# Five normed blocks handed to the FFN by 32x32 turns and transfers, on a one-core two-layer trunk

## The chip, the core and the metric

The kernel runs on one core of a Trainium2 chip. It has a matrix engine (TensorE, PE in the rows; PEld is its weight load), VectorE (DVE), ScalarE (ACT), GpSimd (POOL) and SyncE (SP), which here issues most transfers. Each engine runs its own instructions in order and waits on semaphores. The metric is the device time of one execution in microseconds (us), lower is better.

## The reference

Two layers over 512 tokens of width 1024, float32. Layer 0 mixes tokens by an mLSTM, layer 1 by sliding-window attention; each is followed by a gated FFN with a short causal convolution. Norms stand before and behind every sub-layer:

```
for i in range(2):
    z = rmsnorm(h, norm_mix_pre[i])
    z = mlstm_mixer(z, ...) if i == 0 else swa_sink_mixer(z, ...)   # ends in "@ w_out"
    h = h + rmsnorm(z, norm_mix_post[i])
    z = conv_ffn(rmsnorm(h, norm_ffn_pre[i]), w_up, conv_w, conv_b, w_down)   # u = z @ w_up, then conv, silu, "@ w_down"
    h = h + rmsnorm(z, norm_ffn_post[i])
```

What matters here is the step from a mixer's output product to `rmsnorm(h, norm_ffn_pre[i])` and to the first columns of `@ w_up`.

## The kernel before

The 512 tokens are four blocks of 128 (`NB = 4`), the width is eight tiles of 128 (`KT = 8`). Each float32 product is made of three rounded ones: an operand is kept as a rounded part (`act_hi`, `w_hi`) and the rest (`act_lo`, `w_lo`); ScalarE makes the rounded part and VectorE subtracts it from the source. TensorE contracts over partitions, so an input of a projection must have its features on the partitions. A norm leaves tokens on the partitions. Each normed block `zn[:, b % 2]` (128 tokens by 1024 features) is therefore turned on TensorE: eight 128x128 matmuls against the identity, into two PSUM banks, from where `act_hi[:, :, block]` is rounded and `act_lo[:, :, block]` split.

Behind the mLSTM, `out_block(c, ...)` (matmuls at L1690 to L1692) makes the output products of block c; `turn_norm` (L1507) turns block c-1 between its parts, `norm_post`, `norm_pre` and `norm_hi` on ScalarE and `norm_post`, `norm_pre` (L958) and `norm_lo` (L964) on VectorE make the norms of block c-1. Block c+2's products wait until block c is split, since they use its banks. The FFN then starts with four units of 128 columns over the first 256 tokens (L1498 to L1500), which need blocks 0 and 1; block 3 is turned behind the third of them (`turn_last`), and the second 256 tokens follow when all four blocks are there.

Behind the attention the same is done in half turns of four matmuls (`turn`, L1884; `turn_hi` L863, `turn_lo` L1419). The order is a list of steps, `block_work(s)`, for 16 steps of four heads, two steps a pair `m`, and a last list behind them. "out" is a quarter of a block's output product, "y" the bias (`add_bias`, L952, on VectorE) and the square for the norm, "post" and "pre" the two norms, "turn" a half turn. Every engine goes through the same list and does its own part of each entry, so the order in the list is the order in each engine's queue. In a pair TensorE makes scores, mixes values for the pair before (`mix`), turns probabilities (`turn_probs`, L1851) and puts output parts between them (`filling`). Probabilities are scaled on GpSimd (L545) once VectorE has the reciprocal of their sum (`inverse`).

SP loads the FFN's weights by `ffn_loads(l)`: four units ahead, then a loop whose loads each wait until a unit's buffer is free (L427).

Of the kernel before, what the change touches and what calls it, by code (L numbers as in the profile page):

```python
# [39 lines left out]
def trunk(nc, x, x_turned, columns, m_w_in, m_gate_bias, m_w_out, a_w_in, a_sinks, a_w_out,  # L40
# [68 lines left out]
    with ExitStack() as ctx:  # L109
# [117 lines left out]
        out_done = sem("out_done")  # L227
        warm_in = sem("warm_in")
# [46 lines left out]

        def products(n):


            last = [G_MOUT + KT, G_DOWN[0] + FT, G_AOUT + KT, G_DOWN[1] + FT][n // NB] - 1
            return (w_used, counted(last)) if n % NB == NB - 1 else (y_done, n - n // NB + 1)  # L280
# [5 lines left out]
        def block_work(s):  # L286
            c, i = s // ASTEPS, s % ASTEPS
            if c < NB:
                return {0: [("y", c - 2), ("out", c - 1, 0), ("turn", c - 3, 1)],
                        1: [("out", c - 1, 1), ("post", c - 2)],  # L290
                        2: [("out", c - 1, 2), ("pre", c - 2)],
                        3: [("turn", c - 2, 0), ("out", c - 1, 3)]}[i]
            return [("y", NB - 2), ("out", NB - 1, 0), ("post", NB - 2), ("out", NB - 1, 1),
                    ("pre", NB - 2), ("turn", NB - 3, 1), ("out", NB - 1, 2), ("turn", NB - 2, 0),
                    ("turn", NB - 2, 1), ("out", NB - 1, 3), ("y", NB - 1), ("post", NB - 1),
                    ("pre", NB - 1), ("turn", NB - 1, 0), ("turn", NB - 1, 1)]

        AT_STEPS = NB * ASTEPS
        WORK = [[w for w in block_work(s) if w[1] >= 0] for s in range(AT_STEPS + 1)]
# [46 lines left out]
        def _(sp):  # L346
# [67 lines left out]

            def ffn_loads(l):
                up, down = G_UP[l], G_DOWN[l]
                w_up = f_w_up[l].rearrange("(k p) n -> p k n", p=P)
                for j in range(4):
                    load_free(up + j)
                    tile = FT * (j % 2) + j // 2  # L420
                    load(up + j, w_up[:, :, tile * P:(tile + 1) * P],
                         raw[:, j].rearrange("p (k c) -> p k c", k=KT))
                with sp.Fori(1, FT // 2) as i:
                    for j in range(4):
                        sp.wait_ge(w_lo_done, i * 4 + counted(up + j - 4))
                        tile = i * 2 + (FT * (j % 2) + j // 2)
                        nc.sync.dma_start(raw[:, j].rearrange("p (k c) -> p k c", k=KT),  # L427
                                          w_up[:, :, bass.ds(tile * P, P)]).then_inc(raw_in[j], 16)
# [122 lines left out]
        def _(act):  # L551
# [41 lines left out]

            def norm_hi(n, b, bank):

                act.wait_ge(zt_done, n - NB + 1)
                nc.scalar.copy(act_hi[:, :, b * P:(b + 1) * P],
                               ps[:, bank:bank + 2].rearrange("p a (k t) -> p (a k) t", t=P))\
                    .then_inc(z_hi, 1)
# [119 lines left out]
            for c in range(NB):  # L719
                if c >= 2:  # L720
                    norm_hi(NB + c - 2, c - 2, 4 + 2 * (c % 2))
                if c >= 1:
                    norm_post(c - 1, c - 1, 4 + 2 * ((c - 1) % 2))
                    if c == NB - 1:
                        split_hi(G_UP[0])
                if c >= 1:
                    norm_pre(NB + c - 1, c - 1)
                    if c + 1 < NB:
                        gated_hi(c + 1, 0)
                        gated_hi(c + 1, 1)  # L730
            for n in range(1, 4):
                split_hi(G_UP[0] + n)
            norm_hi(2 * NB - 2, NB - 2, 4)
            norm_post(NB - 1, NB - 1, 6)
            norm_pre(2 * NB - 1, NB - 1)
            norm_hi(2 * NB - 1, NB - 1, 6)
# [141 lines left out]
            for m in range(A_PAIRS):  # L878
# [13 lines left out]
                for s in (2 * m, 2 * m + 1):  # L892
# [3 lines left out]
                    if s + 2 < AT_STEPS:  # L896
                        probs(s + 2)
            for w in pair_work(A_PAIRS - 1, "turn"):
                work(w)
            work(("y", NB - 2))  # L900
            mixed_hi(AT_STEPS // 2 - 1)
            for w in WORK[AT_STEPS][1:]:
                work(w)
                if w == ("turn", NB - 3, 1):
                    split_hi(G_UP[1])
# [11 lines left out]
        def _(dve):  # L917
# [43 lines left out]
            def norm_lo(n, b, bank):  # L961

                dve.wait_ge(z_hi, n - NB + 1)
# [3 lines left out]
                                        ALU.subtract).then_inc(z_lo, 1)  # L967

# [254 lines left out]
            for c in range(NB):  # L1223
                if c >= 2:
                    norm_lo(NB + c - 2, c - 2, 4 + 2 * (c % 2))
# [16 lines left out]
            for n in range(1, 4):  # L1242
                split_lo(G_UP[0] + n)
            norm_lo(2 * NB - 2, NB - 2, 4)
            norm_post(NB - 1, NB - 1, 6)
            norm_pre(2 * NB - 1, NB - 1)
            norm_lo(2 * NB - 1, NB - 1, 6)
# [186 lines left out]
            def work(w):  # L1434
# [6 lines left out]
                elif w[0] == "pre":  # L1441
                    norm_pre(3 * NB + w[1], w[1])

            inverse(0)
            for m in range(A_PAIRS):
# [25 lines left out]
                if m + 1 < A_PAIRS:  # L1471
                    inverse(2 * m + 2)
            for w in pair_work(A_PAIRS - 1, "turn"):
                work(w)
            for w in WORK[AT_STEPS]:
# [3 lines left out]
                if w == ("turn", NB - 3, 1):  # L1479
                    split_lo(G_UP[1])  # L1480
                    split_lo(G_UP[1] + 1)
# [10 lines left out]
        def _(pe):  # L1492
# [212 lines left out]
            for c in range(NB):  # L1705
                if c == 0:
                    turn_heads(1)
                if c >= 2:
                    pe.wait_ge(z_lo, c - 1)
# [5 lines left out]
                if c >= 1:  # L1715
# [75 lines left out]
            def norm_blocks(n):  # L1791
                pe.wait_ge(z_lo, n)
# [4 lines left out]
            for n, lo, hi in [(n, 0, S // 2) for n in range(4)] + [(n, S // 2, S) for n in range(4)] \  # L1797
                    + [(n, 0, S) for n in range(4, 6)]:
                g = G_AIN + n
                pe.wait_ge(z_lo, NB + hi // P)  # L1800
# [131 lines left out]
            for m in range(A_PAIRS):  # L1932
                if m + 1 < A_PAIRS:
                    scores(2 * m + 3)
                    scores(2 * m + 2)
                if m >= 1:
                    mix(m - 1)
                filling(m, 0)
# [12 lines left out]
            def turned_blocks(n):  # L1951
                pe.wait_ge(t_lo, len(TURNS) - 2 * (NB - n))
# [42 lines left out]
```

## Time and profile before

| | |
|---|---|
| median of 3 runs | 1093.57 us (1093.29 to 1093.6) |
| the profiled execution | 1094.01 us |
| its span, first to last instruction | 1091.9 us |
| TensorE busy | 1085.2 us (99%) |
| VectorE, ScalarE, GpSimd busy | 535.5, 428.7, 50.3 us |
| granted TensorE clock, mean | 0.999 of full |
| transfers | 109.51 MB, 32.7% of 16 engines on SP's queue |

The busy times overlap. Matmuls are pipelined, so the durations of neighbours overlap too, and what one costs is read from the distance between starts. Times in the timelines are from the start of the span.

### The profile page before, as it was taken

To read this page: it belongs to the slowest core of one execution; us is meant where nothing else is said; L and a number is where in the kernel's file an instruction comes from. 1 tells how busy PE (TensorE), PEld (TensorE's weight loads), DVE (VectorE), ACT (ScalarE), POOL (GpSimd) and SP (SyncE) were. 2 spreads that over 40 slices of the span, in tenths; PEclk is the share of its full clock that TensorE was granted. 3 is DMA by queue.
4 is the path that set the end of the run, shared out by engine and by line. 5 is a ranking of instruction groups with operands and counts; after the bars stand their busy time and mean duration, and the time that the engine had idled before them with its cause. 6 is when DMAs were issued, how large, how long until landed. Compare 5 with 4: busy or idle time off the path is not lost.

```text
span 1091.9 us, 14755 instructions
## 1 busy us (share of the span) xinstructions
PE 1085.2 (99%) x5550; PEld 910.3 (83%) x5550; DVE 535.5 (49%) x807; ACT 428.7 (39%) x748; POOL 50.3 (5%) x51
## 2 busy tenths in 40 slices
PE   9999999999999999999999999999999999999998
PEld 8888888898888888888889987789888888888886
DVE  7544578644343434333366587564343434523344
ACT  6511456543232323222355376653323232422242
POOL 1100211000000000000000024200000000000000
PEclk9999999999999999999999999999999999999999
DMA  9332326222324232122272542022333333312231
GB/s 287 106 106 79 114 86 224 77 74 82 115 77 115 77 115 77 39 96 96 96 193 59 154 97 78 2 78 84 108 87 105 88 105 91 101 36 99 95 136 77
DMA packets 141764, 109.51 MB, mean 100 GB/s; under 512 B 22480, under 2 KB 127088, under 8 KB 141728
## 3 DMA queue, kind: packets, MB, share of 16 engines
q1 hardware_dynamic: 140720, 105.84, 32.7%
q0 software_dynamic: 864, 2.92, 0.9%
q8 instruction: 25, 0.41, 0.2%
q10 hardware_dynamic: 144, 0.26, 0.1%
q14 instruction: 11, 0.09, 0.0%
HBM read 106.87 MB, written 2.13 MB: 100 GB/s over the span
## 4 chain that ended last, share of the span: by engine, by line
PE 98%; DVE 1%; ACT 0%; issue 0%; DVEq 0%
PE ps L1498 18%; PE ps L1499 18%; PE ps L1500 18%; PE ps L1747 7%; PE ps L1745 7%; PE ps L1746 7%; PE ps L1690 3%; PE ps L1692 3%; PE ps L1691 3%; PE ps L1579 1%; PE ps L1580 1%; PE ps L1581 1%; PE ps L1838 1%; PE ps L1869 1%; PE ps L1851 1%; PE ps L1526 1%
## 5 line engine op out<-in xcount | busy, mean ns | idle before, releaser
L1498 PE MATMUL ps<-act_hi,w_hi 128*128 128x512 f32 (+1 forms) x1016 | 368.7, 363 | 0.1
L1500 PE MATMUL ps<-act_hi,w_lo 128*128 128x512 f32 (+1 forms) x1016 | 366.4, 361 | 0.0
L1499 PE MATMUL ps<-act_lo,w_hi 128*128 128x512 f32 (+1 forms) x1016 | 366.4, 361 | 0.0
L1498 PEld LDWEIGHTS ps<-act_hi,w_hi 128*128 128x128 f32 x1016 | 191.7, 189 | 31.3 <-DVE w_lo L929 0.9
L1500 PEld LDWEIGHTS ps<-act_hi,w_lo 128*128 128x128 f32 x1016 | 191.7, 189 | 29.1
L1499 PEld LDWEIGHTS ps<-act_lo,w_hi 128*128 128x128 f32 x1016 | 191.8, 189 | 29.0 <-issue 0.2
L1747 PE MATMUL ps<-w_hi,w_lo 128*128 128x512 f32 x288 | 112.0, 389 | 0.0
L1745 PE MATMUL ps<-w_hi 128*128 128x512 f32 x288 | 112.0, 389 | 0.0
L1746 PE MATMUL ps<-w_lo,w_hi 128*128 128x512 f32 x288 | 112.0, 389 | 0.0
L755 ACT ACTIVATE arena<-ps,vecs 128x512 f32<-128x512 f32 x44 | 34.3, 779 | 188.6 <-PE ps L1500 188.6
L1264 DVE SCALAR_TENSOR_TENSOR arena<-ps,vecs,arena 128x511 f32<-128x511 f32 x44 | 33.0, 750 | 144.4 <-ACT arena L755 144.4
L749 ACT CAST w_hi<-raw 128x1024 fp32r<-128x1024 f32 x80 | 83.1, 1043 | 39.4 <-PE ps L1500 39.4
L1298 DVE TENSOR_TENSOR w_lo<-raw,w_hi 128x1024 fp32r<-128x1024 f32 x32 | 39.2, 1225 | 119.9 <-ACT w_hi L780 119.9
L1256 DVE TENSOR_TENSOR w_lo<-raw,w_hi 128x1024 fp32r<-128x1024 f32 x80 | 94.1, 1218 | 0.2
L564 ACT CAST w_hi<-raw 128x1024 fp32r<-128x1024 f32 x66 | 67.9, 1045 | 64.5 <-PE ps L1581 24.7
L1273 DVE TENSOR_TENSOR arena<-ps,arena 128x512 f32 (+1 forms) x44 | 30.5, 692 | 117.1 <-PE ps L1500 113.5
L929 DVE TENSOR_TENSOR w_lo<-raw,w_hi 128x1024 fp32r<-128x1024 f32 x65 | 78.2, 1219 | 18.7 <-ACT w_hi L564 18.6
L780 ACT CAST w_hi<-raw 128x1024 fp32r<-128x1024 f32 x32 | 33.6, 1050 | 129.3 <-PE ps L1747 129.3
L1746 PEld LDWEIGHTS ps<-w_lo,w_hi 128*128 128x128 f32 x288 | 54.1, 188 | 11.3
L1747 PEld LDWEIGHTS ps<-w_hi,w_lo 128*128 128x128 f32 x288 | 54.1, 188 | 11.2
L1745 PEld LDWEIGHTS ps<-w_hi 128*128 128x128 f32 x288 | 54.1, 188 | 11.2
L759 ACT ACTIVATE arena<-arena 128x512 f32<-128x512 f32 x44 | 27.8, 632 | 79.6 <-DVE arena L1268 79.6
(209 smaller groups left out, 1219.6 us busy)
## 6 DMA issues: line engine op xcount, KB each, us to landing
raw<-in_f_w_up SPq DMA_DIRECT2D x88, 512.0 KB, 4.7
raw<-in_f_w_down SPq DMA_DIRECT2D x44, 512.0 KB, 3.3
raw<-in_m_w_in SPq DMA_DIRECT2D x23, 512.0 KB, 4.1
raw<-in_m_w_out SPq DMA_DIRECT2D x8, 512.0 KB, 3.2
raw<-in_a_w_in SPq DMA_DIRECT2D x16, 256.0 KB, 4.3
raw<-in_a_w_out SPq DMA_DIRECT2D x16, 256.0 KB, 5.1
h<-in_x SPq DMA_DIRECT2D x4, 512.0 KB, 7.4
h<-in_x_turned SPq DMA_DIRECT2D x3, 512.0 KB, 6.7
```

The lines of the kernel that those rows point to most:

```text
L564: nc.scalar.copy(w_hi[:, s], raw[:, s % 4]).then_inc(w_hi_done, 1)
L749: nc.scalar.copy(w_hi[:, 4 + s], raw[:, s]).then_inc(w_hi_done, 1)
L755: nc.scalar.activation(cv[:, t], ps[:, 2 * t], ACT.Identity, scale=taps[l][:, 2, bass.ds(f, 1)], bias=taps[l][:, 3, bass.ds(f, 1)]).then_i ...
L929: nc.vector.tensor_tensor(w_lo[:, s], raw[:, s % 4], w_hi[:, s].bitcast(F32), ALU.subtract).then_inc(w_lo_done, 1)
L1256: nc.vector.tensor_tensor(w_lo[:, 4 + s], raw[:, s], w_hi[:, 4 + s].bitcast(F32), ALU.subtract).then_inc(w_lo_done, 1)
L1298: nc.vector.tensor_tensor(w_lo[:, j], raw[:, j], w_hi[:, j].bitcast(F32), ALU.subtract).then_inc(w_lo_done, 1)
L1498: nc.tensor.matmul(dst, uh[:, k], zh, start=(k == 0), stop=False)
L1499: nc.tensor.matmul(dst, uh[:, k], zl, start=False, stop=False)
L1500: ins = nc.tensor.matmul(dst, ul[:, k], zh, start=False, stop=(k == KT - 1))
L1745: nc.tensor.matmul(dst, hi[:, bs], w_hi[:, s, hs], start=start, stop=False)
L1746: nc.tensor.matmul(dst, hi[:, bs], w_lo[:, s, hs], start=False, stop=False)
L1747: return nc.tensor.matmul(dst, lo[:, bs], w_hi[:, s, hs], start=False, stop=stop)
```

## The change

Blocks 0 to 2 behind the mLSTM and blocks 0 and 1 behind the attention (`MOVED`) are no longer turned on TensorE. VectorE turns each 32x32 piece of the block in place (`turn_squares`); SP then moves the 32-row bands to their places with 16 transfers from SBUF to SBUF of 32 partitions by 8 by 32 floats each (`move`), straight into the block's columns of `act_lo`; ScalarE rounds them into `act_hi` (`moved_round`) and VectorE subtracts (`moved_rest`). The transfers stand in SP's queue behind the first four FFN loads and ahead of the loop. Block 3 of the mLSTM side and blocks 2 and 3 of the attention side go as before.

In the attention's last list the last output part comes ahead of block 2's two turns, and in the last pair the first filling part comes ahead of `mix`. ScalarE and VectorE take the first FFN unit's weights (`split_hi`, `split_lo`) earlier in the list, and the second's behind `moved_round` and `moved_rest`. The FFN's first half waits for `moved_lo`.

```diff
+        MOVED = [(0, 0), (0, 1), (0, 2)][:3] + [(2, 0), (2, 1)][:2]
+        FIRST_MOVED = 3
@@ block_work, the last list
             return [("y", NB - 2), ("out", NB - 1, 0), ("post", NB - 2), ("out", NB - 1, 1),
-                    ("pre", NB - 2), ("turn", NB - 3, 1), ("out", NB - 1, 2), ("turn", NB - 2, 0),
-                    ("turn", NB - 2, 1), ("out", NB - 1, 3), ("y", NB - 1), ("post", NB - 1),
+                    ("pre", NB - 2), ("out", NB - 1, 2), ("out", NB - 1, 3), ("turn", NB - 2, 0),
+                    ("turn", NB - 2, 1), ("y", NB - 1), ("post", NB - 1),
                     ("pre", NB - 1), ("turn", NB - 1, 0), ("turn", NB - 1, 1)]
-        WORK = [[w for w in block_work(s) if w[1] >= 0] for s in range(AT_STEPS + 1)]
+        WORK = [[w for w in block_work(s) if w[1] >= 0 and (w[0] != "turn" or (2, w[1]) not in MOVED)]
+                for s in range(AT_STEPS + 1)]
@@ SP
+            def move(src, dst, t0, landing):
+                for i in range(4):
+                    for j in range(4):
+                        nc.sync.dma_start(dst[32 * j:32 * j + 32, :, t0 + 32 * i:t0 + 32 * i + 32],
+                                          src[32 * i:32 * i + 32, :, 32 * j:32 * j + 32]).then_inc(landing, 16)
+            def move_squares(n):
+                b = MOVED[n][1]
+                sp.wait_ge(sq_turned, n + 1)
+                move(zn[:, b % 2].rearrange("p (k c) -> p k c", k=KT), act_lo[:].bitcast(F32), b * P,
+                     moved_in[n])
@@ ffn_loads, behind the first four loads
+                for n in range(FIRST_MOVED, len(MOVED)) if l else range(FIRST_MOVED):
+                    move_squares(n)
@@ ScalarE
+            def moved_round(n):
+                bs = slice(MOVED[n][1] * P, (MOVED[n][1] + 1) * P)
+                act.wait_ge(moved_in[n], 16 * 16)
+                nc.scalar.copy(act_hi[:, :, bs], act_lo[:, :, bs].bitcast(F32)).then_inc(moved_hi, 1)
@@ ScalarE behind the mLSTM
             for c in range(NB):
-                if c >= 2:
-                    norm_hi(NB + c - 2, c - 2, 4 + 2 * (c % 2))
...
+                if c == 2:
+                    moved_round(0)
             for n in range(1, 4):
                 split_hi(G_UP[0] + n)
-            norm_hi(2 * NB - 2, NB - 2, 4)
+                if n == 1:
+                    moved_round(1)
             norm_post(NB - 1, NB - 1, 6)
             norm_pre(2 * NB - 1, NB - 1)
+            moved_round(2)
             norm_hi(2 * NB - 1, NB - 1, 6)
@@ ScalarE in the attention
+                if m == A_PAIRS - 2:
+                    moved_round(FIRST_MOVED)
...
             mixed_hi(AT_STEPS // 2 - 1)
+            split_hi(G_UP[1])
             for w in WORK[AT_STEPS][1:]:
                 work(w)
-                if w == ("turn", NB - 3, 1):
-                    split_hi(G_UP[1])
+                if w == ("post", NB - 2):
+                    moved_round(FIRST_MOVED + 1)
                     split_hi(G_UP[1] + 1)
@@ VectorE
+            def turn_squares(n):
+                half, b = MOVED[n]
+                dve.wait_ge(zn_done, half * NB + b + 1)
+                nc.vector.transpose(zn[:, b % 2], zn[:, b % 2]).then_inc(sq_turned, 1)
+            def moved_rest(n):
+                bs = slice(MOVED[n][1] * P, (MOVED[n][1] + 1) * P)
+                dve.wait_ge(moved_hi, n + 1)
+                nc.vector.tensor_tensor(act_lo[:, :, bs], act_lo[:, :, bs].bitcast(F32),
+                                        act_hi[:, :, bs].bitcast(F32), ALU.subtract).then_inc(moved_lo, 1)
@@ VectorE behind the mLSTM
+                if 1 <= c <= FIRST_MOVED:
+                    turn_squares(c - 1)
+                if c == 2:
+                    moved_rest(0)
+            moved_rest(1)
-            for n in range(1, 4):
+            for n in range(1, 3):
                 split_lo(G_UP[0] + n)
-            norm_lo(2 * NB - 2, NB - 2, 4)
             norm_post(NB - 1, NB - 1, 6)
+            split_lo(G_UP[0] + 3)
             norm_pre(2 * NB - 1, NB - 1)
+            moved_rest(2)
@@ VectorE in the attention
                 elif w[0] == "pre":
                     norm_pre(3 * NB + w[1], w[1])
+                    if (2, w[1]) in MOVED:
+                        turn_squares(FIRST_MOVED + w[1])
...
                 if m + 1 < A_PAIRS:
                     inverse(2 * m + 2)
+                if m == A_PAIRS - 2:
+                    moved_rest(FIRST_MOVED)
...
                 if w == ("post", NB - 2):
                     mixed_lo(AT_STEPS // 2 - 1)
-                if w == ("turn", NB - 3, 1):
                     split_lo(G_UP[1])
+                if w == ("pre", NB - 2):
+                    moved_rest(FIRST_MOVED + 1)
                     split_lo(G_UP[1] + 1)
@@ TensorE
                 if c >= 2:
-                    pe.wait_ge(z_lo, c - 1)
+                    pe.wait_ge(h_done, c - 1)
...
-                if c >= 1:
+                if c >= FIRST_MOVED + 1:
                     turn_norm(NB + c - 1, c - 1, 10 - bank)
...
             def norm_blocks(n):
-                pe.wait_ge(z_lo, n)
+                pe.wait_ge(moved_lo, min(n, FIRST_MOVED))
+                if n == NB:
+                    pe.wait_ge(z_lo, NB - FIRST_MOVED)
...
+                if m == A_PAIRS - 1:
+                    filling(m, 0)
                 if m >= 1:
                     mix(m - 1)
-                filling(m, 0)
+                if m < A_PAIRS - 1:
+                    filling(m, 0)
...
             def turned_blocks(n):
-                pe.wait_ge(t_lo, len(TURNS) - 2 * (NB - n))
+                pe.wait_ge(moved_lo, len(MOVED))
+                if len(TURNS) > 2 * (NB - n):
+                    pe.wait_ge(t_lo, len(TURNS) - 2 * (NB - n))
```

## Rows read from the trace of the kernel before

**Rows 1.** The page's busy times by engine: us, share of the span, instructions.

```profile
PE 1085.2 (99%) x5550; PEld 910.3 (83%) x5550; DVE 535.5 (49%) x807; ACT 428.7 (39%) x748; POOL 50.3 (5%) x51
```

**Rows 2.** The page's chain that ended last, shares by engine.

```profile
PE 98%; DVE 1%; ACT 0%; issue 0%; DVEq 0%
```

**Rows 3.** Timeline, TensorE, mLSTM output: start, length (us), engine, line, operation, shape.

```profile
185.92 0.39 PE L1692 MATMUL ps<-w_hi,act_lo 128*128 128x512 f32 x1
186.15 1.03 PE L1507 MATMUL ps<-ident,arena 128*128 128x128 f32 x8
186.94 0.48 PE L1690 MATMUL ps<-w_hi,act_hi 128*128 128x512 f32 x1
...
189.57 0.39 PE L1692 MATMUL ps<-w_hi,act_lo 128*128 128x512 f32 x1
...
193.65 0.39 PE L1692 MATMUL ps<-w_hi,act_lo 128*128 128x512 f32 x1
```

**Rows 4.** The same, from the mLSTM output into the FFN.

```profile
214.30 0.28 PE L1498 MATMUL ps<-act_hi,w_hi 128*128 128x256 f32 x1
...
222.94 1.04 PE L1507 MATMUL ps<-ident,arena 128*128 128x128 f32 x8
```

**Rows 5.** The same, attention's last pairs and the start of its FFN.

```profile
687.04 0.60 PE L1884 MATMUL ps<-ident,arena 128*128 128x128 f32 x4
687.39 0.48 PE L1690 MATMUL ps<-w_hi,act_hi 128*128 128x512 f32 x1
...
707.73 1.05 PE L1851 MATMUL ps<-ident,arena 128*128 128x128 f32 x8
...
718.05 0.60 PE L1884 MATMUL ps<-ident,arena 128*128 128x128 f32 x4
...
721.26 1.03 PE L1884 MATMUL ps<-ident,arena 128*128 128x128 f32 x8
...
724.87 0.28 PE L1498 MATMUL ps<-act_hi,w_hi 128*128 128x256 f32 x1
...
733.74 1.09 PE L1884 MATMUL ps<-ident,arena 128*128 128x128 f32 x8
```

**Rows 6.** SP's issues by line: ns min/median/max, first and last start us.

```profile
L427 SPq DMA_DIRECT2D raw<-in_f_w_up x80: 372/373/388, 208.4 to 926.6; - x80
...
L381 SPq DMA_DIRECT2D arena<-in_m_w_in x1: 468/468/468, 6.0 to 6.0; - x1
...
L351 SPq DMA_DIRECT2D raw<-in_f_w_up x8: 384/1382/4459, 171.8 to 658.0; - x8
```

**Rows 7.** The output stores of line 474, issue to landing.

```profile
DMA to landing us min/median/max: 2.0/2.6/2.6
```

**Rows 8.** Packets, 13.5 to 14 (32-byte loads), 555.5 to 563.5 (256-byte loads).

```profile
DMA packets 1069, 0.07 MB, mean 132 GB/s; under 512 B 1053, under 2 KB 1053, under 8 KB 1069
...
DMA packets 6889, 1.75 MB, mean 219 GB/s; under 512 B 6887, under 2 KB 6887, under 8 KB 6887
```

**Rows 9.** Timeline of VectorE behind the mLSTM; brackets: idle before, releaser.

```profile
185.76 1.28 DVE L1179 TENSOR_TENSOR act_lo<-arena,act_hi 128x512 fp32r<-128x512 f32 x2
...
197.35 1.29 DVE L1179 TENSOR_TENSOR act_lo<-arena,act_hi 128x512 fp32r<-128x512 f32 x2
...
208.83 1.28 DVE L958 SCALAR_TENSOR_TENSOR arena<-h,stat,g_pre 128x1024 f32<-128x1024 f32 x1 [0.64 <-ACT stat L571]
```

**Rows 10.** The page's group of the weight casts on ScalarE.

```profile
L564 ACT CAST w_hi<-raw 128x1024 fp32r<-128x1024 f32 x66 | 67.9, 1045 | 64.5 <-PE ps L1581 24.7
```

**Rows 11.** Timeline of VectorE behind the attention.

```profile
705.95 1.27 DVE L958 SCALAR_TENSOR_TENSOR arena<-h,stat,g_pre 128x1024 f32<-128x1024 f32 x1
...
722.53 1.28 DVE L1419 TENSOR_TENSOR act_lo<-ps,act_hi 128x512 fp32r<-128x512 f32 x2
725.07 1.22 DVE L952 TENSOR_TENSOR arena<-ps,arena 128x1024 f32<-128x1024 f32 x1 [1.25 <-PE ps L1692]
```

**Rows 12.** Timeline of GpSimd, the last scaling of probabilities.

```profile
703.24 1.89 POOL L545 TENSOR_TENSOR arena<-arena 128x1024 f32<-128x1024 f32 x1 [1.07 <-DVE arena L1404]
```

More of the change, by code:

```diff
@@ L227, in trunk @@
         out_done = sem("out_done")
+        sq_turned, moved_hi, moved_lo = (sem(n) for n in ("sq_turned", "moved_hi", "moved_lo"))
+        moved_in = [sem(f"moved_in{i}") for i in range(5)]
         warm_in = sem("warm_in")
@@ L274, in turned_in, with through_psum @@
             return xt_in[k if k < 2 else 1 + k // 2], 16
+        MOVED = [(0, 0), (0, 1), (0, 2)][:3] + [(2, 0), (2, 1)][:2]
+        FIRST_MOVED = 3
+        def through_psum(n):
+            return n - NB + 1 - FIRST_MOVED
         def products(n):
@@ L592, in norm_pre @@
                 rsqrt_mean(b, 2).then_inc(rs_pre, 1)
+            def moved_round(n):
+                bs = slice(MOVED[n][1] * P, (MOVED[n][1] + 1) * P)
+                act.wait_ge(moved_in[n], 16 * 16)
+                nc.scalar.copy(act_hi[:, :, bs], act_lo[:, :, bs].bitcast(F32)).then_inc(moved_hi, 1)
             def norm_hi(n, b, bank):
-                act.wait_ge(zt_done, n - NB + 1)
+                act.wait_ge(zt_done, through_psum(n))
                 nc.scalar.copy(act_hi[:, :, b * P:(b + 1) * P],
@@ L961, in norm_lo @@
             def norm_lo(n, b, bank):
-                dve.wait_ge(z_hi, n - NB + 1)
+                dve.wait_ge(z_hi, through_psum(n))
                 nc.vector.tensor_tensor(act_lo[:, :, b * P:(b + 1) * P],
@@ L1223, in _ @@
             for c in range(NB):
-                if c >= 2:
-                    norm_lo(NB + c - 2, c - 2, 4 + 2 * (c % 2))
                 if c == 0:
@@ L1799, in _ @@
                 g = G_AIN + n
-                pe.wait_ge(z_lo, NB + hi // P)
+                pe.wait_ge(z_lo, NB - FIRST_MOVED + hi // P)
                 pe.wait_ge(w_lo_done, counted(g))
```

## The prediction, made before the changed kernel was run

> **What bounds the kernel now.** I read three views, in this order. The page's first part: TensorE is busy 99% of the span and no other engine is at half of it [rows 1]. The chain that ended last: 98% of it is TensorE [rows 2], so an instruction taken off TensorE is worth its own length as long as nothing it needs comes late, and work added on the other engines is free until TensorE waits for it. Then the timelines of the two places that change, to see how much room each hand-over has. In the first, TensorE goes from the last mLSTM output matmul to the first FFN matmul at 214.30 with no gap, and meets block 3's turn at 222.94 [rows 4]. In the second it starts the FFN at 724.87 and comes to block 3's turns at 733.74 [rows 5]. Three half units of FFN last 8.64 us (214.30 to 222.94), so in the second place the turns could have begun at 733.51: about 0.2 us of waiting for block 3's norm is already there. That wait is where I expect most of the attention side's gain to go.
>
> All times "before" below are of the profiled execution. Its span is 1091.9 us and the run itself 1094.01, so 2.1 us lie around the span; the median of the runs is 1093.57, 0.44 less than that run. I take the saving from the span and subtract it from the median.
>
> **The change, part by part.**
>
> *Turns removed behind the mLSTM.* A turn of one block is 8 matmuls against the identity. From 185.92 to 189.57 twelve output matmuls start, with one turn among them; eighteen more without a turn take 189.57 to 193.65, 0.2267 us each [rows 3]. Twelve would be 2.72, the stretch is 3.65, so a turn costs 0.93: 0.79 until the next matmul and 0.14 in the slower starts after the switch. Three go: 2.8 us. TensorE then reaches the FFN at 214.30 - 2.8 = 211.5.
>
> *What must be there at 211.5.* The FFN's first half needs blocks 0 and 1 rounded and split. Block 1's path in the new kernel: its norm ran behind its out products, which end 0.93 earlier (one turn gone). VectorE's last split of gated heads behind it ended at 197.35 + 1.29 = 198.64 [rows 9], now 197.7. The 32x32 turn appears nowhere in the trace of before; I price it as a pass over the same 128x1024 fp32 in SBUF or PSUM, 1.22 [rows 11], bounds 1.1 and 2.4 (two passes): ends 198.9. Then SP issues 16 transfers. An issue that waits for nothing takes 0.373 over 80 cases, 0.468 at the longest for short runs [rows 6], and I allow 0.05 to the next: 0.42 each, bounds 0.42 and 0.52. The last starts at 199.0 + 15 x 0.42 = 205.3 (206.8 at the upper bound). Landing: nothing SBUF to SBUF is in the trace; the nearest are the output stores from SBUF, 2.0 to 2.6 [rows 7], so it lands at 207.3, at most 209.4. ScalarE rounds it in 1.05 [rows 10]: it comes to it behind block 2's norm and one weight cast, which is 208.83 - 1.86 + 1.05 = 208.0 [rows 9, 10], so 208.0 to 209.1, at most 210.5. VectorE takes the rest in 1.22, and ahead of that in its queue stands block 2's own turn, which follows 208.83 - 1.86 + 1.28 = 208.25 and ends at 209.5. So block 1 is ready at 210.7; TensorE comes at 211.5. Room 0.8; at the upper bound of issue and landing together 211.7, a wait of 0.2. I take no wait.
>
> *The queues behind these.* Block 0's turn follows 185.76 + 1.28 [rows 9] and ends at 188.3; its 16 issues are through at 195.0, before block 1's begin, and ScalarE's wait for its landing (197 to 199) stands ahead of block 2's norm, which starts when its products end, one out block (48 matmuls, 10.9) ahead of the FFN: 200.6. Block 2's issues run from 209.5 to 216.2 and land by 219; they are needed when the fourth half unit is through, 211.5 + 8.64 + 0.93 + 2.88 = 224.0, after 2.3 us of rounding and splitting. The loads of the FFN's fifth unit on stand behind block 2's issues on SP, so they go out at 216.2 instead of as soon as the first unit is split. The loop that needs them begins after eight half units, 211.5 + 23.0 + 0.9 = 235: covered by 19 us. ScalarE and VectorE exchange a copy out of PSUM for one out of SBUF of the same size. Sum of this side: -2.8.
>
> *Turns removed behind the attention.* Four half turns of 4 matmuls: 687.04 to 687.39 is 0.35 [rows 5], and the one at 718.05, which stands alone between wide matmuls, carries some 0.1 more: 1.5 us together. The part of the output that is moved ahead in the last pair costs nothing: it stands where TensorE would otherwise wait for the turned probabilities, since it comes 0.7 earlier. Block 0's turn on VectorE follows its norm in an idle stretch, and its transfers have over 7 us. Its rounding and rest, however, stand in the queues ahead of the last reciprocal: GpSimd's last scaling of probabilities began at 703.24 and took 1.89 [rows 12]; with 1.05 and 1.22 put ahead and 0.35 to 0.5 gained it begins at about 705.1 and ends at 707.0. TensorE wanted its result at 707.73 [rows 5], now at 707.0: a wait of 0 to 0.2; I take 0. Block 1's scaling ended at 705.95 + 1.27 [rows 11], now some 0.15 later behind the longer copy on ScalarE; its turn ends at 708.6, its transfers land by 717.0 to 718.5, round and rest end by 721, and the FFN starts at 723.3: room 2.
>
> *Block 3's chain, late in the new order.* The last output part now comes ahead of block 2's turns. So it ends earlier, at 724.87 - 1.5 - 0.9 = 722.4, and the turns follow. But on VectorE block 2's two splits still stand ahead of block 3's bias add, and now they wait for turns that run after the part. Before, the splits began 1.27 after the turns (721.26 to 722.53), each 0.6, and the bias add at 725.07 came 0.2 behind the part's end [rows 5, 11]. Now the add begins at 722.4 + 1.27 + 1.2 = 724.9, 2.5 behind it. From its start to block 3's turn on TensorE it was 733.74 - 725.07 = 8.67, all one chain of dependent passes that the change leaves as it is. So the turn begins at 733.6, where TensorE would be at 722.4 + 0.9 + 8.64 = 731.9: a wait of 1.6. The attention side gives 733.74 - 733.6, about 0.2, of its 1.5. Behind that turn nothing differs.
>
> Sum: 2.8 + 0.2 = 3.0 off the span. 1093.57 - 3.0 = 1090.6.
>
> **A rule that speaks against it.** Packets in the trace: 32-byte ones drained at 1069 in 0.5 us, 7.5 ns for each of 16 engines; 256-byte ones at 6887 in 8 us, 18.6 ns [rows 8]. A block is 4096 runs of 128 bytes, 256 for an engine: 1.9 to 4.8 us by these, less than the 6.7 of the issues, so the issues bind. The Trainium skill (DMA: Bandwidth & Descriptors, Specifications) says that below 512 bytes a transfer is done as a read-modify-write; another section of that page (Why small descriptors are slow (HBM only)) exempts SBUF to SBUF. No run here shows which holds for such a move; what it would give as a mechanism is the second rival.
>
> **The rivals.**
> 1. *Block 3's chain isn't late*: the wait of 1.6 is absent, because the splits or the add run sooner than I have them. Then the attention side gives its 1.5 and the old 0.2: 1093.57 - 2.8 - 1.7 = 1089.1. Against it: the queue order is fixed and the 8.67 are measured. 0.12.
> 2. *Packets bind*: each 128-byte run costs twice the 256-byte one, 37 ns; 256 of them are 9.5 us a block. Block 1 is then through at 199.0 + 9.5, lands at 210.5, and with 1.05 and 1.22 is ready at 212.8: TensorE waits 1.3. Behind the attention the room of 2 holds. 1091.9; with longer landings up to 1093. For it: a path of which the trace has no row; against it: the fast 32-byte row. 0.20.
> 3. *The issues are held back, and it gets slower.* SP's issues of the first FFN weights took 1.38 at the median and 4.46 at most where much was outstanding [rows 6]. Sixteen short transfers in flight could do the same. Block 1 is ready at 188.4 + 31x + 2.0 + 2.3 for x us an issue; the 3.0 are eaten at about x = 0.7, slower from there. At x = 1.0 TensorE waits 12 us behind the mLSTM, and behind the attention 708.7 + 15 + 4.3 - 723.3 = 4.7: about 1107. Against it: 80 issues of 1024 runs each went out at 0.373, and from the first four weight loads to 208.4 none are issued [rows 6]. 0.10.
>
> **How the numbers follow.** My forecast, 1090.6 (1090.0 to 1091.3), has 0.58. The range takes in rivals 1 and 2: 1089.0 to 1093.4; what is left out is rival 3 and a little of the tails. A difference under 0.2% (2.2 us) can hardly be told from none: faster means under 1091.4. That is the forecast nearly whole, rival 1 and a small part of rival 2: 0.67. Slower, above 1095.8, is rival 3: 0.09. The rest, 0.24, is the same.
>
> **What would show it.** In the profile after: 24 and 16 identity matmuls fewer; 80 issues of 32 KB each at a pitch of about 0.42 with landings of 2 to 2.6; the first FFN matmul at 211.5 with no idle time named before it; the turns of the last attention block preceded by about 1.6 us of idle time put down to VectorE's scaling of block 3, and starting at 733.6 - 2.8 = 730.8 from the span's start. Wrong would be: idle time ahead of the first FFN matmul (rivals 2 and 3, told apart by the issue pitch against the packet times), a pitch over 0.7, a 32x32 turn well over 1.3 us, or no idle time before the last turns (rival 1).

## The result: slower, 1097.1 us, and the profile after

The changed kernel takes 1097.12 us (median of 9 runs, 1095.32 to 1097.73) against 1093.41 (9 runs, 1093.07 to 1093.73) on the same chip: a ratio of 1.003, 95% interval 1.0021 to 1.0039. The forecast was 1090.6, with a range of 1089.0 to 1093.4. The profiled execution took 1097.68, its span is 1095.6, 3.7 more than before.

TensorE did get rid of its 40 matmuls, but the chain of waits is no longer TensorE's alone. Here are the page's busy times and shares of the chain after (for [rows 1, 2]):

```profile
PE 1082.8 (99%) x5510; PEld 907.1 (83%) x5510; DVE 542.8 (50%) x810; ACT 428.4 (39%) x746; POOL 50.8 (5%) x51
...
PE 92%; DVE 3%; ACT 2%; SPq 2%; issue 1%; DMA 0%; DVEq 0%; ACTq 0%
```

And TensorE's waits (line that waits, releasing engine and line: us in total, times, longest):

```profile
PE ps L1557 <- DVE act_lo L1016: 4.0, 2, 3.0
PE ps L1945 <- DVE arena L995: 2.0, 1, 2.0
```

TensorE is busy 2.4 us less and the span is 3.7 longer. The chain now runs through SP's queue (2%), ScalarE and VectorE. L1557 is the first FFN matmul: it waits in both layers for L1016, the second half of the split of the moved blocks. L1945 is the turn of the last attention block.

**Behind the mLSTM.** The timeline of TensorE after, for [rows 4]:

```profile
211.22 0.39 PE L1751 MATMUL ps<-w_hi,act_lo 128*128 128x512 f32 x1
214.58 0.58 PE L1557 MATMUL ps<-act_hi,w_hi 128*128 128x256 f32 x1 [2.96 <-DVE act_lo L1016]
214.96 0.42 PE L1558 MATMUL ps<-act_lo,w_hi 128*128 128x256 f32 x1
215.17 0.41 PE L1559 MATMUL ps<-act_hi,w_lo 128*128 128x256 f32 x1
...
224.73 1.03 PE L1566 MATMUL ps<-ident,arena 128*128 128x128 f32 x8
```

The output part ends where the forecast had it, about 211.5. Then TensorE waits 2.96. After that its matmuls of 256 columns start 0.21 apart up to 217.9, where they started 0.12 apart before, and 0.12 apart again from there on; the three half units up to block 3's turn take 10.15 instead of 8.64. The windows after (PE busy, PEld, DVE, ACT, POOL, granted clock, DMA share, GB/s) show why:

```profile
200.00:210.00 10.00, 10.00 (x46) 8.29 (x45) 7.40 (x6) 6.07 (x11) 0.00 (x0) 1.00 0.28 45
210.00:215.00 5.00, 2.04 (x10) 1.42 (x9) 1.70 (x2) 2.78 (x3) 0.00 (x0) 0.94 0.31 51
215.00:220.00 5.00, 5.00 (x33) 5.00 (x33) 4.92 (x5) 2.25 (x6) 0.00 (x0) 0.72 0.29 48
220.00:225.00 5.00, 5.00 (x44) 5.00 (x44) 3.02 (x3) 2.11 (x5) 0.00 (x0) 1.00 0.54 128
```

The granted clock is 1.00 up to the wait, 0.72 in the five microseconds behind it (part of them at the lower of its two levels) and 1.00 again: another 1.5 us on top of the wait. What came late is read from the answer on the line of SP's moves (ns minimum, median, maximum of all 80, for [rows 6, 7]):

```profile
L429 SPq DMA_DIRECT2D act_lo<-arena x80: 585/611/1968, 188.1 to 722.3; - x80
DMA to landing us min/median/max: 1.9/1.9/3.4
```

and from the timeline of block 1: VectorE's turn, SP's first, longest and last issue, ScalarE's rounding, VectorE's rest:

```profile
197.53 1.24 DVE L1010 STREAM_TRANSPOSE arena<-arena 128x1024 f32<-128x1024 f32 x1
...
198.79 0.59 SPq L429 DMA_DIRECT2D act_lo<-arena  x1
206.97 1.97 SPq L429 DMA_DIRECT2D act_lo<-arena  x1
210.29 0.61 SPq L429 DMA_DIRECT2D act_lo<-arena  x1
...
212.22 1.04 ACT L624 CAST act_hi<-act_lo 128x1024 fp32r<-128x1024 f32 x1 [4.29 <-DMA act_lo<-arena]
...
213.30 1.23 DVE L1016 TENSOR_TENSOR act_lo<-act_lo,act_hi 128x1024 fp32r<-128x1024 f32 x1 [3.71 <-ACT act_hi L624]
```

The 32x32 turn (1.24), the landing (1.9 at the median; from the last issue at 210.29 to the rounding at 212.22 it is 1.93) and the two passes behind it (1.04 and 1.23) are as priced. The issues aren't: 0.611 each, 0.65 from one to the next, but for one step of 1.05 (201.38 to 202.43) and one issue of 1.97 among the sixteen. From the first start to the last they take 11.5 us.

**Behind the attention.** TensorE enters this stage about 2.3 late. It could have started the first FFN at 211.45, 2.85 sooner than before; it started 3.13 after that (2.96 of them idle), and the clock took 1.51, which makes 1.8 at block 3's turn (224.73 against 222.94). Of the other 0.5, 0.3 comes at a turn behind the first FFN (575.83 against 573.72 before), which now waits 0.15 for VectorE's norm, and 0.2 early in the attention; the reason wasn't followed further. TensorE, SP's first and last issue of block 1, ScalarE and VectorE, for [rows 5, 11]:

```profile
726.60 0.39 PE L1557 MATMUL ps<-act_hi,w_hi 128*128 128x256 f32 x1 [1.05 <-DVE act_lo L1016]
737.45 1.09 PE L1945 MATMUL ps<-ident,arena 128*128 128x128 f32 x8 [1.95 <-DVE arena L995]
...
711.53 0.58 SPq L429 DMA_DIRECT2D act_lo<-arena  x1
722.32 0.61 SPq L429 DMA_DIRECT2D act_lo<-arena  x1
...
724.24 1.05 ACT L624 CAST act_hi<-act_lo 128x1024 fp32r<-128x1024 f32 x1 [5.23 <-DMA act_lo<-arena]
...
708.35 1.87 DVE L995 SCALAR_TENSOR_TENSOR arena<-h,stat,g_pre 128x1024 f32<-128x1024 f32 x1
725.32 1.22 DVE L1016 TENSOR_TENSOR act_lo<-act_lo,act_hi 128x1024 fp32r<-128x1024 f32 x1 [4.99 <-ACT act_hi L624]
727.60 1.28 DVE L1473 TENSOR_TENSOR act_lo<-ps,act_hi 128x512 fp32r<-128x512 f32 x2
728.79 1.22 DVE L989 TENSOR_TENSOR arena<-ps,arena 128x1024 f32<-128x1024 f32 x1
```

The same sixteen issues take 10.8 us here. The FFN waits 1.05 for block 1. The rest of block 1 (725.32), a weight split behind it and block 2's two splits (727.60) stand in VectorE's queue ahead of block 3's bias add (728.79), and the last turns wait another 1.95. From the add to the turns it is 728.79 to 737.45, 8.66: the chain that the forecast carried over as 8.67. This stage adds 1.4 (2.3 late at its entry, 3.71 at the last turns): waits of 1.05 and 1.95, less the 1.5 of the turns and the 0.2 that was waited before, make 1.3 of it.

### The profile page after: what moved, and what is told of

The parts are those of the page before. It is cut to its first block, busy times and chain, and to the rows that moved or that the text cites. A ratio compares the mean times of both kernels' runs of the same rounds, so it can differ in the third digit from the quotient of the medians.

```text
span 1095.6 us, 14754 instructions
## 1 busy us (share of the span) xinstructions
PE 1082.8 (99%) x5510; PEld 907.1 (83%) x5510; DVE 542.8 (50%) x810; ACT 428.4 (39%) x746; POOL 50.8 (5%) x51
## 4 chain that ended last, share of the span: by engine, by line
PE 92%; DVE 3%; ACT 2%; SPq 2%; issue 1%; DMA 0%; DVEq 0%; ACTq 0%
PE ps L1557 18%; PE ps L1558 18%; PE ps L1559 18%; PE ps L1805 7%; PE ps L1804 7%; PE ps L1806 7%; SPq L429 2%; PE ps L1749 2%; PE ps L1751 2%; PE ps L1750 2%; PE ps L1638 1%; PE ps L1639 1%; PE ps L1640 1%; PE ps L1899 1%; PE ps L1912 1%; PE ps L1930 1%
## 5 line engine op out<-in xcount | busy, mean ns | idle before, releaser
L1557 PE MATMUL ps<-act_hi,w_hi 128*128 128x512 f32 (+1 forms) x1016 | 369.6, 364 | 4.1 <-DVE act_lo L1016 4.0
L1557 PEld LDWEIGHTS ps<-act_hi,w_hi 128*128 128x128 f32 x1016 | 192.4, 189 | 35.9 <-DVE act_lo L1016 4.7
```

What stands on the lines that cost most here:

```text
L1557: nc.tensor.matmul(dst, uh[:, k], zh, start=(k == 0), stop=False)
```

## The experiments

**1. Half of the transfers.** Both sides keep their turns, waits, roundings and order, but only 8 of a block's 16 transfers are issued (the half of each block that belongs to the upper 64 partitions isn't brought over).

```
-                    for j in range(4):
+                    for j in range(2):
...
-                act.wait_ge(moved_in[n], 16 * 16)
+                act.wait_ge(moved_in[n], 16 * 8)
```

> Every second of the 16 transfers of a block is left out (so half of each moved block holds other data; 40 issues in place of 80), nothing else. Theory: SP's issues, 0.66 us from start to start, set when a moved block lands. With 8 of them a block lands about 5.3 us sooner: no wait ahead of either FFN start, the granted clock stays up, and what is left is the wait of about 1.6 us ahead of the last attention block's turns, which the order of VectorE's queue makes. Time about 1090.6, first FFN matmul at 211.5. Rival A: the landing itself or the rounding and splitting behind it are late: the waits shrink by little, time about 1096. Rival B: the moves are not what costs, the new order in the attention is: time above 1094 though no wait is left behind the mLSTM.

Measured: 1090.57 (1090.22 to 1091.08, 10 runs), ratio 0.9974 (0.9965 to 0.9984). TensorE's first FFN matmul and the last turns:

```profile
211.41 0.28 PE L1557 MATMUL ps<-act_hi,w_hi 128*128 128x256 f32 x1
...
730.71 0.55 PE L1945 MATMUL ps<-ident,arena 128*128 128x128 f32 x3 [1.44 <-DVE arena L995]
```

The window that was at 0.72 in the changed kernel:

```profile
215.00:220.00 5.00, 5.00 (x44) 5.00 (x43) 4.36 (x4) 2.59 (x5) 0.00 (x0) 1.00 0.79 213
```

With a row of issues no longer than the forecast had it (8 x 0.65 = 5.2 us, forecast 6.7), what the forecast says of TensorE comes true: FFN at 211.41 (211.5), no wait, clock 1.00, last turns at 730.71 behind a wait of 1.44 (730.8 and 1.6), time 1090.57 (1090.6). This alone doesn't tell issue time from amount of data; experiment 6 does.

**2. What an issue costs.** The kernel before, with groups of small transfers put ahead of the second FFN's loads, on SP and on GpSimd, where nothing waits for them.

```
+                    probe([(pb[bands[j], :, 0:32], pa[bands[3 - j], :, 0:32]) for j in range(4)])
...
+                        nc.gpsimd.dma_start(pb[bands[j], :, 0:32], pa[bands[3 - j], :, 0:32]).then_inc(pq_done, 16)
```

> The kernel before, with extra transfers that nothing uses, put on SP while it is idle in the attention (behind the first four loads of the second FFN) and four on GpSimd. Groups of four, each waited for: SBUF to SBUF of 32 partitions by 8 by 32 floats (the move); the same bytes as one run of 1 KB a partition; 32 partitions by 32 floats; the move's pattern on 128 partitions (three, one by one); SBUF to DRAM and DRAM to SBUF of the move's pattern; the move's pattern issued by GpSimd. If the pattern (three dimensions on both sides) makes the issue 0.61 us, the 1 KB runs and the 32 by 32 take some 0.35 to 0.45 and all three-dimensional ones 0.6, DRAM or not. If two SBUF sides make it, the DRAM ones take 0.37 to 0.45 and all SBUF to SBUF ones 0.6. If 32 partitions make it, the 128-partition one takes about 0.4. Landing 1.9 for all. The time stays within 1 us of the kernel before.

Measured: 1093.23 (one run). Issues by line, ns minimum, median, maximum (L433 is SP, L576 GpSimd):

```profile
L433 SPq DMA_DIRECT2D arena<-raw x15: 507/592/732, 674.1 to 692.0; - x15
L433 SPq DMA_DIRECT2D p_dram<-raw x4: 609/612/617, 694.6 to 696.6; - x4
L433 SPq DMA_DIRECT2D arena<-p_dram x4: 579/608/609, 698.7 to 700.6; - x4
...
L576 POOL DMA_DIRECT2D arena<-raw x4: 584/588/681, 670.4 to 672.2; - x4
```

Three of the fifteen are the move's pattern on 128 partitions, each issued by itself after the one before it had landed; the first and the last of them:

```profile
685.42 0.70 SPq L433 DMA_DIRECT2D arena<-raw  x1
692.00 0.59 SPq L433 DMA_DIRECT2D arena<-raw  x1
```

Some 0.6 for every shape tried (each issue between 0.51 and 0.73), within SBUF, out to DRAM and back, and on GpSimd too, so that none of the three explanations in the expectation holds. The price is there in a quiet stretch, with no more than four in flight: what is queued isn't needed to make the issues of the changed kernel that long. Nor is the row: the three that stood alone cost as much.

**3. TensorE kept busy through the wait.** Fourteen extra matmuls of 512 columns, whose result nobody reads, ahead of the wait at the first FFN.

```
+                if n < NB:
+                    pe.wait_ge(h_done, NB - 1)
+                    for _ in range(14):
+                        nc.tensor.matmul(ps[:, 4], w_hi[:, 3, 0:P], w_hi[:, 3, 0:HALF], start=True, stop=True)
                 pe.wait_ge(moved_lo, min(n, FIRST_MOVED))
```

> The changed kernel, with 14 matmuls of 512 columns (3.2 us, into a bank that is free, their result unused) ahead of the wait at the first FFN start, where TensorE was idle for 3.0 us and the granted clock stood at 0.93 and then 0.72 in the stretches after. Theory: the idle stretch lowers the clock, and that costs about 1.5 us on top of the wait in the runs where it happens. With the fill the FFN starts within 0.3 us of 214.6 as before, the clock stays at 1.00, and the time is 1095.3 to 1095.7 in every run. Rival: the clock falls for another reason (the transfers, the rounding): time as the changed kernel's, 1095.3 to 1097.7.

Measured: 1097.56 (1096.01 to 1097.72, 5 runs), ratio 1.0034 (1.002 to 1.0049); the expectation missed. Windows behind the mLSTM and at the last turns:

```profile
215.00:220.00 5.00, 5.00 (x44) 5.00 (x43) 4.56 (x4) 2.23 (x7) 0.00 (x0) 1.00 0.31 51
...
735.00:740.00 5.00, 4.03 (x22) 4.03 (x23) 2.23 (x3) 2.46 (x3) 0.00 (x0) 0.67 0.38 108
```

At the first place the expectation held: with the wait filled the clock stays at 1.00 and block 3's turn is reached 8.63 after the FFN's start, not 10.15. But now it falls at the second place, behind the waits of 1.6 and 1.9 there, where it had stayed at 1.00 in the changed kernel's trace. In this trace, filling one wait didn't give the clock's 1.5 us back, since it fell behind another. The one of the five runs with a mean granted clock of 1.000 took 1096.0.

**4 and 5. Each side alone.** The attention as before with the mLSTM side changed (4), and the other way round (5): in each, the other side's queue orders, waits and turns are those of the kernel before.

```
-        MOVED = [(0, 0), (0, 1), (0, 2)][:3] + [(2, 0), (2, 1)][:2]
+        MOVED = [(0, 0), (0, 1), (0, 2)][:3] + [(2, 0), (2, 1)][:0]
...
+        MOVED = [(0, 0), (0, 1), (0, 2)][:0] + [(2, 0), (2, 1)][:2]
+        FIRST_MOVED = 0
```

> Only the mLSTM side of the change; the attention is as in the kernel before. Theory (16 issues one behind the other at 0.66 us make block 1 late, TensorE waits 3 us ahead of the first FFN matmul and its clock is lower after that wait): in the changed kernel the attention was entered 2.3 us later than before, so 1093.4 + 2.3 = 1095.7 (1095.0 to 1096.3), with the wait of 2.5 to 3.5 at the first FFN matmul and a granted clock under 0.8 just behind it. Rival (the loss is made at the attention; the mLSTM side pays for itself): 1093.4 or less.

> Only the attention side of the change; the blocks behind the mLSTM are turned on TensorE as in the kernel before. Theory (the same pitch makes block 1 of the attention late too, by about 1 us at the second FFN, and that pushes block 3's bias add on VectorE, so that TensorE waits 2 us before the last turns): in the changed kernel 1.4 us were added behind the attention's entry, so 1093.4 + 1.4 = 1094.8 (1094.2 to 1095.4). Rival (the attention side loses only because the first side comes before it, by a lowered clock or a shift): my forecast for this side, 1093.4 - 0.2 = 1093.2, with no wait at the first FFN matmul.

Measured: 1095.59 (1094.18 to 1096.33, 10 runs) for the mLSTM side, ratio 1.0017 (1.0007 to 1.0027); 1095.26 (1094.61 to 1096.6, 10 runs) for the attention side, ratio 1.0017 (1.0008 to 1.0027). Experiment 4's windows behind the mLSTM, where TensorE waited 2.8 for block 1:

```profile
210.00:215.00 5.00, 2.17 (x10) 1.67 (x10) 2.56 (x3) 3.64 (x4) 0.00 (x0) 0.87 0.32 53
215.00:220.00 5.00, 5.00 (x36) 5.00 (x36) 4.58 (x4) 2.22 (x7) 0.00 (x0) 0.79 0.31 50
```

Experiment 5's two waits, and its window at the last turns:

```profile
PE ps L1937 <- DVE arena L993: 2.0, 1, 2.0
PE ps L1551 <- DVE act_lo L1014: 1.0, 1, 1.0
```

```profile
735.00:740.00 5.00, 5.00 (x32) 5.00 (x31) 1.29 (x2) 2.21 (x3) 0.00 (x0) 0.66 0.07 22
```

Each side loses by itself, about 2.0 and 1.7 us. Both theories held and both rivals fell: the attention side makes its waits of 1.0 and 2.0 with no change ahead of it, and the clock can fall behind a wait at either place. That the two losses add up to the 3.7 of the whole is in part chance: each side's trace holds a fall of the clock of its own, the trace of the whole only one.

**6. The same transfers, issued by two queues.** Nothing left out; GpSimd, which has nothing to do behind the mLSTM, issues 8 of the 16 transfers of the blocks that are urgent.

```
+                move(nc.sync, n, range(2 if n in BY_POOL else 4), moved_in[n])
...
+            for n in range(FIRST_MOVED):
+                pool.wait_ge(sq_turned, n + 1)
+                move(nc.gpsimd, n, range(2, 4), moved_pool[n])
...
+                if n in BY_POOL:
+                    act.wait_ge(moved_pool[n], 16 * 8)
```

> The whole change with nothing left out, but of every block that is urgent (0, 1, 2 behind the mLSTM and 1 behind the attention) GpSimd issues 8 of the 16 transfers while SP issues the other 8; block 0 of the attention stays on SP. Theory (the issue pitch of one queue is the term I had too small): the issues take 8 x 0.66 = 5.3 us a block as in the run with half of the transfers, no wait at the first FFN matmul, about 1.4 us of waiting left before the last turns, 1090.6 (1090.2 to 1091.2). Rival (the transfers themselves or their landing are what is slow; a second queue doesn't help, and the run with half of the transfers was quick because it moved half of the data): 1095 to 1097 with the wait still at the first FFN matmul. Second rival (GpSimd's issues are much slower than its 0.6 in the price run while VectorE works): between the two.

Measured: 1090.19 (1089.89 to 1090.9, 7 runs), ratio 0.9969 (0.9957 to 0.998). The moves on both queues:

```profile
L240 SPq DMA_DIRECT2D act_lo<-arena x48: 585/611/1953, 188.1 to 712.6; - x48
L240 POOL DMA_DIRECT2D act_lo<-arena x32: 584/584/681, 188.4 to 711.0; - x32
```

And the one wait at these places that is left, ahead of the last turns:

```profile
PE ps L1955 <- DVE arena L1005: 1.4, 1, 1.4
```

The issues on SP are no shorter, but each queue has half of an urgent block's, and the whole of the data goes through. No wait at either FFN, and the forecast's time. So it was the time of one queue's issues and not the transfers. The Trainium skill (DMA: Bandwidth & Descriptors, Issuing engines are not separate DMA queues) says that a second issuing engine saves only the time to initiate a DMA, usually small against the DMA itself. That it saves this and nothing else agrees with the rows; small it isn't here, 16 issues of 0.61 before a landing of 1.9.

**7. And the bias add first.** As 6, and on VectorE block 3's bias add ahead of the two splits of block 2's turns, the split of the third weight tile ahead of both (the expectation calls it the fourth), and ScalarE rounds that tile earlier too.

```
+            order = [w for w in WORK[AT_STEPS] if w[0] != "turn" or w[1] != NB - 2]
+            at = order.index(("y", NB - 1)) + 1
+            order[at:at] = [("turn", NB - 2, half) for half in range(2)]
+            for w in order:
```

> As the run with two queues, and on VectorE block 3's bias add stands ahead of the two splits of block 2's turns, with the split of the fourth up weights pulled ahead of both. Theory (the last wait before the turns is the queue order on VectorE that the forecast named): the wait of 1.4 us goes, 1090.6 - 1.4 = 1089.2 (1088.9 to 1089.8). Rival (the chain from the add to the turns is stretched by the work that I put elsewhere, or another wait takes its place): 1090.6 as without the new order.

> The run with two queues and block 3's bias add first, once more with more rounds: 1088.2 to 1088.9, no wait of TensorE over 0.3 us at either FFN's start or before the last turns.

Measured: 1088.45 (1088.21 to 1088.87, 4 runs), ratio 0.9953 (0.9936 to 0.997); again, 1088.63 (1088.24 to 1089.25, 5 runs), 0.9957 (0.9943 to 0.9971). Block 3's add and the last turns in the first of the two:

```profile
719.35 1.22 DVE L998 TENSOR_TENSOR arena<-ps,arena 128x1024 f32<-128x1024 f32 x1 [0.79 <-PE ps L1762]
...
728.67 0.60 PE L1956 MATMUL ps<-ident,arena 128*128 128x128 f32 x4
```

The add now waits for nothing but its products, the turns stand without idle time before them, and 1.6 to 1.7 us come off (1.4 expected, so that the first of the two times lies below the 1088.9 to 1089.8 of its expectation). This is the version that beats both kernels, by 4.5 to 5.2 us against the one before.

**8. Which shapes cost 0.6.** The kernel before again, with groups of four in six shapes.

> The kernel before with a probe on SP ahead of the second FFN's loads: groups of four issues one behind the other, with a wait for their landing between groups. In order: DRAM to SBUF with 416 bytes for each of 128, of 64 and of 32 partitions; SBUF to SBUF with 416 bytes for each of 128; DRAM to SBUF with 8 runs of 48 bytes for each of 128; SBUF to SBUF with the same. Theory A (an issue that follows another at once costs about 0.6 us when a transfer covers fewer than all 128 partitions, as the half-width loads of the attention's output weights in the kernel before did, and 0.43 when it covers all): 0.35 to 0.48 in the groups 1, 4, 5 and 6, about 0.6 in 2 and 3. Theory B (every issue that follows another at once costs 0.6 unless it is large): about 0.6 in all six. Theory C (SBUF as the source costs): 0.6 in 4 and 6 alone.

Measured: 1093.28 (one run). An issue out of each of the six groups in their order, ahead of that of the third group the first of its four:

```profile
662.56 0.43 SPq L433 DMA_DIRECT2D arena<-in_f_w_up  x1
667.45 0.60 SPq L433 DMA_DIRECT2D arena<-in_f_w_up  x1
669.63 0.33 SPq L433 DMA_DIRECT2D arena<-in_f_w_up  x1
670.93 0.42 SPq L433 DMA_DIRECT2D arena<-in_f_w_up  x1
674.40 0.60 SPq L433 DMA_DIRECT2D arena<-raw  x1
679.32 0.67 SPq L433 DMA_DIRECT2D arena<-in_f_w_up  x1
685.27 0.68 SPq L433 DMA_DIRECT2D arena<-raw  x1
```

None of the three theories holds: 0.43 for 128 partitions, 0.60 for 64 and 0.42 for 32 out of DRAM; 0.60 out of SBUF where DRAM gave 0.43; 0.67 and more with many short runs from either (up to 0.81). Within a group the first issue is the shortest (0.33 and then 0.42 in the third group), but for the first group, whose first took 1.73. What sets the price of a shape stays open; behind the first of a group it lay between 0.42 and 0.81.

## Why the prediction was wrong

**The step that failed is the issue time** in "What must be there at 211.5": 0.42 each, bounds 0.42 and 0.52, last start 6.3 us behind the first. It is 0.65 apart, one issue in the block took 1.97, and the last start is 11.5 behind the first. That is 5.2 more; with the landing 0.1 shorter and the first issue 0.2 sooner block 1 comes 4.9 later. The forecast had a slack of 1.1 in the path (VectorE wasn't to be free before 209.5, the transfers alone would have allowed 208.4) and 0.8 of room in front of TensorE; what is left is the wait of 3.0. The bound was drawn from the wrong rows. The 80 issues at 0.373 [rows 6] are loads of 512 KB that each stand alone in a loop, 1.1 us or more from one start to the next. Experiments 2 and 8 show what each of these two differences is worth: the place in a row some 0.1 (0.33 against 0.42), the kind of transfer the larger part, since issues of the move's pattern on 128 partitions, standing alone, took 0.59 to 0.70. The trace of before had issues of another kind that follow one another; this row of it, the half-width loads of the attention's output weights, wasn't read:

```profile
L465 SPq DMA_DIRECT2D raw<-in_a_w_out x16: 466/596/1588, 617.9 to 640.4; - x16
```

0.596 at the median, and one of 1.588. Sixteen of those, 0.64 apart with one long one, come within a microsecond of the changed kernel's block. That this kind and the moves cost the same is a finding, not something the trace of before could have shown.

**A term was missing: what a wait does to the clock.** The forecast and the second and third rivals price a wait at its own length. The wait of 2.96 cost 1.5 more, in matmuls at a granted clock of 0.72 over the next five microseconds. The spread goes with the clock: in two of the changed kernel's nine runs the mean granted clock is 1.000, and they took 1095.3 and 1095.5; the others, at 0.998 and 0.999, 1096.5 to 1097.7. The Trainium skill (TensorE: Matmul & The Clock Gate, Part 1: The HAM clock gate) has TensorE's clock fall to half after idleness; the rows agree that it falls behind such waits (0.21 instead of 0.12 between matmuls), and show that it doesn't behind each.

**The point at which it turns** was the third rival's, with a chance of 0.10. It had the effect right, issues that come too late, and set the break-even at 0.7 us an issue. Its reason, issues held back by what is outstanding, isn't what experiment 2 shows: they cost 0.6 with no more than four in flight. At 0.65 its own formula has block 1 ready at 212.9, a wait of 1.4, and 1092.0 in the end. The 5.1 that are missing from the measured time are about: 1.4 for the one long issue and 0.4 for the step of 1.05 in the same row, 1.5 for the clock, 1.05 and 0.35 at the second FFN and its last turns, 0.5 between the first FFN and the attention's last pairs, whose cause stays open.

**The second rival**, the packets, isn't seen. It wanted 9.5 us of transfers a block. With the DMA engines busy 0.28 of the time from 200 to 210, the 11.5 us of a block's issues hold about 3.2 us of them, an estimate from these two numbers; a landing takes 1.9 us at the median, and two queues halve the time. The rule that was weighed (the Trainium skill, DMA: Bandwidth & Descriptors, Specifications: a read-modify-write below 512 bytes) would, at the rival's price, have shown in these moves of 128-byte runs within SBUF, and doesn't. The section Why small descriptors are slow (HBM only) of that page of the Trainium skill leaves SBUF to SBUF out of the slowness of small descriptors, which agrees with the runs; it doesn't speak of the read-modify-write, so the forecast reads more into it than it says.

**The first rival** didn't happen: block 3's chain was late, as forecast, 1.44 in experiment 1. In the changed kernel itself it was later still, since block 1's rest came late into the same queue. Experiment 7 takes the wait away by the order of the queue alone.

**Right, with their numbers:** a turn at 0.93 (TensorE through at 211.45, forecast 211.5), the 32x32 turn at 1.24 (1.22), the landing at 1.9 (2.0), round and rest at 1.05 and 1.23, the output part in the last pair at no cost, the chain from add to turns at 8.66 (8.67), and the sum of it all once the issues are short: 1090.57 and 1090.19 against 1090.6. That the sum comes out so closely is in part luck. In experiment 1 TensorE is 2.9 ahead of the kernel before when it ends the mLSTM's output, but only 2.6 at the turn behind the first FFN (571.14 against 573.72), a loss that the forecast put at nothing; the attention side then gives 0.5 instead of 0.2 (730.71 against 733.74 at the last turns). On the attention side block 1 was forecast to land by 717.0 to 718.5 and did at 724.24, 721.9 without the shift of 2.3: the issues once more, and 0.6 by the norm pass of VectorE ahead of the turn, which took 1.87 (708.35) instead of 1.28 beside GpSimd's scaling (707.25 to 709.14 in this trace).

## What to carry to other kernels

Work that goes from TensorE to many small transfers moves onto the issuing queue, and there the price is the time from one issue to the next in an unbroken row of issues of that kind (sizes, runs, partitions, memories): look for such a row in the trace, or measure one, instead of taking the median of large loads that stand alone, and split the row over an idle queue when it is on the way. Price a wait of the bound engine at more than its length: what the clock loses behind it can come on top, 1.5 us behind the wait of 2.96 here. When work is taken out ahead of a chain, look at what stands before that chain's first instruction on its own queue; putting block 3's add first was worth as much as the four half turns.

## What the runs showed of the hardware

- An issue on SP took 0.373 us (median of 80) for the FFN's up weights, 512 KB each, where it stood alone, and mostly 0.42 to 0.68 for smaller transfers in a row, depending on the shape: 128, 64 and 32 partitions of 416 bytes each out of DRAM gave 0.43, 0.60 and 0.42. GpSimd issued the same moves at 0.584, and the two queues didn't slow one another.
- In every traced run with moves one to three of SP's issues of them took 1.1 to 2.0 us instead of 0.61, at different places in the row; why is open.
- TensorE's granted clock fell behind one wait in each traced run with waits of 1.6 to 3.0 us at these two places (the changed kernel and experiments 3, 4 and 5), and only behind one: 0.72 behind the mLSTM in the changed kernel and 0.79 in experiment 4, 0.67 at the last turns when the first wait was filled, 0.66 there when the first side was undone. With 1.44 as the longest wait there (experiments 1 and 6), or none (7), it stayed at 1.00 in both places. Length alone doesn't tell which wait it falls behind: at the last turns a wait of 1.95 left it at 1.00 in the changed kernel, and one of 1.95 was followed by the fall in experiment 3.
- VectorE turned 128x1024 fp32 in 32x32 squares in 1.24 us, about as long as its plain passes over that size (1.22 and 1.23).
